# Toeplitz bias table and decay sums of a hybrid decoder block spread over partitions through memory instead of by products on TensorE

## The reference, cut to what matters

```python
rel = t_pos[None, :, None] - idx
bias = rel_bias[t5_bucket(rel)].astype(jnp.float32)
logits = logits + jnp.transpose(bias, (0, 1, 3, 2))
```

```python
cs = jnp.cumsum((dt * a).reshape(bsz, n_c, CHUNK, n_h), axis=2)
seg = cs[:, :, :, None, :] - cs[:, :, None, :, :]
decay_ls = jnp.exp(jnp.where(tri[None, None, :, :, None], seg, -jnp.inf))
scores = jnp.einsum("bclhn,bcshn->bclsh", ch, bh).astype(jnp.float32) * decay_ls
```

## Time and profile before

| | us |
|---|---|
| runs | 811.29, 812.05, 813.7 (median 812.05) |
| profiled execution, first to last instruction | 810.0 (its own time is not listed apart) |
| PE busy | 762.2 (94%) |
| DVE busy | 501.6 (62%) |
| ACT busy | 333.9 (41%) |
| POOL busy | 165.3 (20%) |

### The profile page before, as it was taken

The page is one execution under the profiler, slowest core; times in us unless marked ns, Lnnn a source line. Parts: engine busy times, 40 slices in busy tenths (PEclk is TensorE's granted clock), DMA queues, the critical chain, the costliest instruction groups (busy, mean ns, idle before and its releaser), DMA issues.

```text
span 810.0 us, 9558 instructions
## 1 busy us (share of the span) xinstructions
PE 762.2 (94%) x3406; PEld 595.6 (74%) x3406; DVE 501.6 (62%) x753; ACT 333.9 (41%) x491; POOL 165.3 (20%) x128
## 2 busy tenths in 40 slices
PE   3899999999899989979997999999999999999998
PEld 3567777766566667768885788888888888888886
DVE  4236789758779787988867366656655665322222
ACT  5244435465744648435233333443443334211110
POOL 2200433257556434432312000000000000000000
PEclk9999999999899989999998999999999999999999
DMA  8341132311111014111141133323333332322212
GB/s 254 123 155 58 53 104 53 104 53 52 53 52 53 2 52 156 53 53 53 52 131 53 52 104 104 103 83 81 95 104 104 104 104 98 109 104 90 72 47 104
DMA packets 78048, 69.47 MB, mean 86 GB/s; under 512 B 5815, under 2 KB 64535, under 8 KB 78015
## 3 DMA queue, kind: packets, MB, share of 16 engines
q1 hardware_dynamic: 77871, 68.51, 27.4%
q10 hardware_dynamic: 144, 0.52, 0.2%
HBM read 66.91 MB, written 2.12 MB: 85 GB/s over the span
## 4 chain that ended last, share of the span: by engine, by line
PE 79%; DVE 11%; issue 4%; ACT 3%; POOL 2%; DMA 1%; DVEq 0%; POOLq 0%; ACTq 0%
PE bank L1437 67%; PE bank L1443 3%; PE bank L1575 3%; PE bank L1594 2%; DVE u_acc L551 2%; DVE w_lo L561 2%; POOL stats L711 2%; DVE xbcT L1230 1%; PE bank L1552 1%; PE bank L1643 1%; DMA x_in<-in_x 1%; DVE h_lo L1073 1%; PE bank L1560 1%; PE bank L1617 1%; ACT xbcT L924 1%
## 5 line engine op out<-in xcount | busy, mean ns | idle before, releaser
L1437 PE MATMUL bank<-h_hi,w_hi 128*128 128x512 f32 x496 | 200.3, 404 | 1.8 <-DVE h_lo L1073 1.8
L1437 PE MATMUL bank<-h_lo,w_hi 128*128 128x512 f32 x496 | 196.0, 395 | 0.0
L1437 PE MATMUL bank<-h_hi,w_lo 128*128 128x512 f32 x496 | 195.4, 394 | 0.0
L561 DVE TENSOR_TENSOR w_lo<-w_raw,w_hi 128x1408 fp32r<-128x1408 f32 (+1 forms) x34 | 71.3, 2098 | 82.2 <-ACT w_hi L817 82.1
L1437 PEld LDWEIGHTS bank<-h_hi,w_hi 128*128 128x128 f32 x496 | 94.9, 191 | 36.9 <-issue 16.8
L1437 PEld LDWEIGHTS bank<-h_hi,w_lo 128*128 128x128 f32 x496 | 94.7, 191 | 20.4
L1437 PEld LDWEIGHTS bank<-h_lo,w_hi 128*128 128x128 f32 x496 | 95.0, 192 | 18.8
L1398 DVE SCALAR_TENSOR_TENSOR f<-bank,prm,f 128x511 f32<-128x511 f32 x88 | 65.8, 747 | 57.1 <-ACT f L1042 50.8
L817 ACT ACTIVATE w_hi<-w_raw 128x2048 fp32r<-128x2048 f32 x34 | 64.9, 1910 | 77.9 <-PE bank L1437 77.9
L551 DVE SCALAR_TENSOR_TENSOR u_acc<-u_in,prm,u_acc 128x511 f32<-128x511 f32 (+29 forms) x90 | 86.2, 996 | 0.7
L1042 ACT ACTIVATE f<-bank,prm 128x512 f32<-128x512 f32 x44 | 33.8, 769 | 101.2 <-PE bank L1437 101.2
(11 more groups left out here) (220 smaller groups left out, 1140.3 us busy)
## 6 DMA issues: line engine op xcount, KB each, us to landing
w_raw<-in_w_up SPq DMA_DIRECT2D x44, 512.0 KB, 4.5
w_raw<-in_w_in SPq DMA_DIRECT2D x34, 512.0 KB, 4.4
w_raw<-in_w_down SPq DMA_DIRECT2D x22, 512.0 KB, 4.2
w_raw<-in_w_out SPq DMA_DIRECT2D x12, 512.0 KB, 4.2
x_in<-in_x SPq DMA_DIRECT2D x4, 512.0 KB, 6.8
trev<-distance_table SPq DMA_DIRECT2D x1, 2048.0 KB, 8.2
x<-in_x SPq DMA_DIRECT2D x4, 512.0 KB, 6.5
out_x<-y_out SPq DMA_DIRECT2D x8, 256.0 KB, 2.0
```

The costliest lines, as they stand in the source:

```text
L561: eng.tensor_tensor(wlo[:, slot, cols], wraw[:, slot, cols], whi[:, slot, cols].bitcast(F32), ALU.subtract).then_inc(ready, 1)
L1437: ins = pe.matmul(o, a, b, start=first and i == 0 and q == 0, stop=last and i == n - 1 and q == 2)
```

## The change

The bias rows are now made on all 128 partitions at once: `relx` repeats each head's column 16 times (an ACT copy), the product is 128 rows tall, and ACT stores each partition's 640 values eight times, 128 x 8 x 640 (2.6 MB), from its own DMA queue. One read with a row step of NG - 1 from offset P - 1 gives the table the right way round, straight into `tbias` (2 MB, slot 9, issued by ACT). `trev`, `jrev`, the eight products and the eight copies go.

`cs` moves from slot 62 to slot 20, with a third product that gives the sums as rows (32 x 128); DVE copies them, ACT stores them (16 KB), and per chunk SP reads them back with a partition step of 0 (`csl`, 512 KB each) into `dec`, which is now doubled; `sct` is written over `dec`. The `csr` products go; the subtraction on DVE reads `dec` in SBUF instead of a bank.

The diff, cut to its core:

```diff
+CSL_SLOTS = (64, 64, 70, 74)
...
     put(1, ("gtab",))
-    for h in range(NH):
-        put(11 + h, ("tbias", h))
+    put(9, ("tbias",))
+    put(20, ("cs",))
...
-    put(s0, ("silux",), ("cs",))
+    put(s0, ("silux",))
...
+    for t, n in enumerate(CSL_SLOTS):
+        put(n, ("csl", t))
     for t, n in enumerate(SSD_SLOTS):
-        put(n, ("csr", t))
...
-                elif s[0] == "gtab":
...
-                    sp.dma_start(gdram, gsb[:, :]).then_inc(s_gout, 16)
-                    sp.wait_ge(s_gout, 16)
...
-                    src = bass.AP(gdram.tensor, 0, [[1, P], [NG, NH], [1, 512]])
-                    sp.dma_start(trev[:, :, :], src).then_inc(s_trev, 16)
+                elif s[0] == "csl":
+                    t = s[1]
+                    sp.wait_ge(s_cst, 16)
+                    if t < 2:
+                        finished(sp, "pv", NT - 1)
+                    else:
+                        finished(sp, "yd", t - 2)
+                    src = bass.AP(cdram.tensor, SH * P * t, [[0, P], [P, SH], [1, P]])
+                    sp.dma_start(dec[:, t % 2, :, :], src).then_inc(s_csr[t], 16)
...
                 elif k == "gtab":
+                    act.wait_ge(s_oneh, 32)
+                    act.activation(relx[:, :].rearrange("b (h c) -> b h c", h=NH),
+                                   relb[:, :].unsqueeze(2).to_broadcast([NBUCKET, NH, P // NH]),
+                                   ACT.Copy).then_inc(relx_ready, 1)
...
+                    act.dma_start(gdram, gsb[:, :].unsqueeze(1).to_broadcast([P, NH, NG]))\
+                        .then_inc(s_gout, 16)
...
                 elif k == "tbias":
-                    finished(act, *s)
-                    drain(act.activation(tbias[:, s[1], :], ps(*s)[:, :], ACT.Copy), *s)
+
+                    act.wait_ge(s_gout, 16)
+                    act.wait_ge(xn_ready, NT)
+                    src = bass.AP(gdram.tensor, P - 1, [[NG - 1, P], [P * NG, NH], [1, 512]])
+                    act.dma_start(tbias[:, :, :], src).then_inc(s_tbias, 16)
...
                 elif k == "cs":
                     act.wait_ge(csx_ready, 1)
                     act.activation(ecs, csx, ACT.Exp).then_inc(ecs_ready, 1)
+                    evacuated(act, "cs")
+                    act.dma_start(cdram, csT[:, :]).then_inc(s_cst, 16)
...
-                        d = dec[:, 4 * g:4 * g + 4, :]
-                        finished(dve, "csr", t, g)
+                        d = dec[:, t % 2, 4 * g:4 * g + 4, :]
+                        dve.wait_ge(s_csr[t], 16)
...
-                        drain(dve.tensor_tensor(
-                            d, ps("csr", t, g)[:, :].rearrange("p (h l) -> p h l", h=4),
-                            csx[:, c:c + 4].unsqueeze(2).to_broadcast([P, 4, P]), ALU.subtract),
-                            "csr", t, g)
-                        evacuated(dve, "csr", t, g)
+                        dve.tensor_tensor(d, d, csx[:, c:c + 4].unsqueeze(2).to_broadcast([P, 4, P]),
+                                          ALU.subtract).then_inc(segx_ready, 1)
...
-                elif k == "csr":
-                    t = s[1]
-                    for g in range(SG):
-                        claim(pe, "csr", t, g)
-                        for h in range(4):
-                            c = SH * t + 4 * g + h
-                            ins = pe.matmul(ps("csr", t, g)[:, P * h:P * h + P],
-                                            dta[:, c:c + 1].to_broadcast([P, P]), tri[:, :],
-                                            start=True, stop=True)
-                        ins.then_inc(aux_done, 1)
```

More of the change, by code:

```diff
@@ L241, in make_groups @@
         k = s[0]
-        if k in ("prm", "tbias", "idx", "score", "turn", "ln", "lnT", "qkT", "cs", "iwT",
+        if k in ("prm", "idx", "score", "turn", "ln", "lnT", "qkT", "cs", "iwT",
                  "yT"):
@@ L328, in build @@
     w_in, w_out, w_up, w_down = w_in[0], w_out[0], w_up[0], w_down[0]
-    gdram = nc.dram_tensor("distance_table", (NH, NG), F32, kind="Internal").ap()
+    gdram = nc.dram_tensor("distance_table", (P, NH, NG), F32, kind="Internal").ap()
+    cdram = nc.dram_tensor("decay_rows", (NT * SH, P), F32, kind="Internal").ap()
     with ExitStack() as ctx:
@@ L377, in build @@
         relb = at("relb", [NBUCKET, NH], F32, r7 + 2560)
-        gsb = at("gsb", [NH, NG], F32, r7 + 3 * K)
-        jrev = at("jrev", [P, P], F32, r7 + 6 * K)
-        trev = at("trev", [P, NH, 512], F32, r6)
+        gsb = at("gsb", [P, NG], F32, r7 + 3 * K)
+        relx = at("relx", [NBUCKET, P], F32, r7 + 7 * K)
         tbias = at("tbias", [P, NH, 512], F32, r2)
@@ L413, in build @@
         gssm = at("gssm", [P, 512], F32)
-        dec = at("dec", [P, SH, P], F32, rs)
-        sct = at("sct", [P, SH, P], F32, rs + 4 * K)
+        dec = at("dec", [P, 2, SH, P], F32, rs)
+        csT = at("csT", [NT * SH, P], F32, r7 + 6 * K)
         ssm_hi = at("ssm_hi", [P, 4, SEQ], F32R, r4)
@@ L472, in build @@
                              "head_params_landed", "onehot_landed"))
-        s_gout, s_trev, s_x2, s_yout, s_gm, s_gf = (
-            sem(n) for n in ("gtable_stored", "trev_landed", "x2_landed", "y_stored",
+        s_gout, s_tbias, s_x2, s_yout, s_gm, s_gf = (
+            sem(n) for n in ("gtable_stored", "tbias_landed", "x2_landed", "y_stored",
                              "gm_row_landed", "gf_row_landed"))
@@ L499, in build @@
         csx_ready, ecs_ready = sem("csx_ready"), sem("ecs_ready")
+        s_cst, relx_ready = sem("decay_rows_stored"), sem("relx_ready")
+        s_csr = [sem(f"decay_rows_landed{t}") for t in range(NT)]
+        segx_ready = sem("segx_ready")
         seg_ready, dec_ready, sct_ready = sem("seg_ready"), sem("dec_ready"), sem("sct_ready")
@@ L729, in _ @@
                         finished(pool, "qkT", "k", 3)
-                        for hh in range(NH):
-                            evacuated(pool, "tbias", hh)
+                        pool.wait_ge(s_tbias, 16)
                     if i >= 2:
@@ L840, in _ @@
                         n = 512 if i == 0 else NG - 512
[L841 removed]
+                        drain(act.activation(gsb[:, 512 * i:512 * i + n], ps("gt", i)[:, 0:n],
                                              ACT.Copy), "gt", i)
+                    for i in range(2):
+                        evacuated(act, "gt", i)
+                    act.dma_start(gdram, gsb[:, :].unsqueeze(1).to_broadcast([P, NH, NG]))\
+                        .then_inc(s_gout, 16)
                 elif k == "norm":
@@ L866, in _ @@
                     dst = {"iq": iqT, "v": v_tok, "z": z_tok, "cg": u_acc, "ca": u_in}.get(what)
+                    if (what, i) == ("ca", 3):
+                        act.wait_ge(s_cst, 16)
                     take(dst[:, i, :], what, i)
@@ L1498, in _ @@
                         n = 512 if i == 0 else NG - 512
-                        pe.matmul(ps("gt", i)[0:NH, 0:n], relb[:, :], oneh[:, 512 * i:512 * i + n],
+                        pe.wait_ge(relx_ready, 1)
+                        pe.matmul(ps("gt", i)[:, 0:n],
+                                  relx[:, :],
+                                  oneh[:, 512 * i:512 * i + n],
                                   start=True, stop=True).then_inc(aux_done, 1)
@@ L1642, in _ @@
                         c = slice(SP_ * h, SP_ * h + SP_)
-                        ins = pe.matmul(ps("yd", t)[:, c], sct[:, h, :], xd[:, c], start=True,
+                        ins = pe.matmul(ps("yd", t)[:, c], dec[:, t % 2, h, :], xd[:, c], start=True,
                                         stop=True)
```

40 lines of the change are left out of this document (12 added, 28 removed).

## The result

| | before | after |
|---|---|---|
| median of the runs | 812.88 us (4 runs, 811.29 to 814.04) | 824.23 us (4 runs, 822.16 to 825.19) |
| profiled execution: span | 810.0 us | 823.3 us |
| mean granted clock of it | 0.983 | 0.961 |

What follows compares the result with a forecast made beforehand. PE rarely stops up to 104 us, DVE sets the pace from 104 to 124 and bounds the scan. Terms -0.3 + 1.7 - 1.4 - 0.3 + 0.5 = +0.2 us on 812.05 gave 812.3 us, range 807.5 to 815.7.

Steps and rivals of the forecast that it cites:

- Term 1: Up to k's turn: eight products and copies leave, `cs` in slot 20 gives back 2.5 us; -0.3 us (-2.8 to +0.5).
- Term 2: At the wait for k: PE waits 5 us instead of 3.56, lower clock follows; +1.7 us (0 to +3.1).
- Term 3: Behind the SiLUs: ACT's exponential and its table load leave the chain; -1.4 us (-0.5 to -1.6).
- Term 4: In the scan: the decay products leave PE, mostly lengthening its waits; -0.3 us (0 to -7.2).
- Term 5: In the scan: DVE's subtraction reads SBUF twice, one more delay beside POOL; +0.5 us (0.1 to 2.4).
- rival D: In the scan: the subtraction stands until POOL's instruction ends, 2.4 us in place of 0.5; 814.2 us, chance 0.1.
- At nothing: Table and decay reads and stores, ACT's `relx` copy and POOL's dropped instructions: hidden or in idle time, no cost.
- C: Before q's turn: the new 3.3 us wait lowers the clock too; +3.1 us, 815.4 us, chance 0.17.
- B: Low-clock stretches fall elsewhere after a small shift, dropping one such as that after 216.62; 809.2 us, chance 0.13.
- A: At k: `cs` is covered and the clock holds; -4.0 us, 808.0 us, chance 0.2.

Runs made afterwards that it cites:

- e9: The changed kernel with POOL's waits of e5 and `cs` in slot 30 instead of 20, behind the normalised k; 816.40 us, ratio 1.0059.
- e5: The changed kernel with POOL's three instructions of the second, third and fourth chunk held until that chunk's `seg` is done; 815.92 us, ratio 1.0036.
- e17: The kernel before with one edit, `cs` moved to slot 20, table and decay still by products; 813.74 us, ratio 1.0009.
- e1: The table half of the change alone: bias table by memory, decay sums on PE as before; 813.57 us, ratio 1.0026.
- e4_cs22: The changed kernel with `cs` in slot 22 instead of 20; 817.52 us, ratio 1.0088.

## Why the prediction was wrong

- **Term 1** (-0.3): held as a sum. PE waited 3.34 us before q's turn, which began at 92.58 (said: 3.3 and 92.6), and DVE's scaling for k came at 112.89 (said: 112.8):

```profile
112.89 0.16 DVE L1205 TENSOR_SCALAR stats<-stats 128x32 f32<-128x32 f32 x1
112.96 2.28 DVE L564 TENSOR_TENSOR w_lo<-w_raw,w_hi 128x2048 fp32r<-128x2048 f32 x1
...
120.58 1.89 DVE L1213 TENSOR_TENSOR k_tok<-k_tok,stats 128x512 f32<-128x512 f32 x3 [1.97 <-POOL stats L709]
```

  Its inner piece, 2.5 us for `cs`, is 2.2 by e9 against e5 (112.29 and 114.49). `cs` on ACT is as worked out: exponential, issue, copy, square.

```profile
108.58 0.28 ACT L974 ACTIVATE stats<-stats 128x96 f32<-128x96 f32 x1 [5.74 <-DVE stats L1254]
108.59 0.34 ACTq L976 DMA_DIRECT2D decay_rows<-csT  x1
108.97 0.60 ACT L913 ACTIVATE k_tok<-bank 128x512 f32<-128x512 f32 x1
109.60 0.60 ACT L916 ACTIVATE sq<-bank 128x512 f32<-128x512 f32 x1
```

- **Term 2** (+1.7): the mechanism held, the size was 2.4. PE went on at 123.13 after 4.77 us, 0.24 earlier than before, and slot 28 stands 2.21 later.
- **Term 3** (-1.4): held, -1.3 between slots 60 and 64.
- **Term 4** (-0.3, bounds 0 and -7.2) failed, in its bound. "That wait becomes 3.6 and DVE gains nothing" was right: it became 3.79. But a wait that grows was costed at nothing, a few paragraphs after I had costed one at k by the clock. In the first chunk of the profiled execution it cost 4.3 us (slot 69 at -3.66, slot 70 at +0.65), of which 1.8 is the gain that had to go and the rest the lower level behind the wait. A loss belonged into the range; e17 shows that even an unchanged wait can have it.
- **Term 5** (+0.5, bounds 0.1 and 2.4) is the step that decided: it measured 4.25 us of DVE in `seg`, and holding POOL back was worth 8 us of the time (e5), clock included. I took "one more such delay" from a single long L1257, where rival D counted one delay of 0.8 in each of three chunks. The rule that D rested on was right and D's size was not: it used one POOL instruction for each chunk, while POOL has four in a row, and three of the fourth chunk's four `seg` instructions were caught (+2.8 us; +0.7 in the second and third chunk, as D had it). The `yb` row of 1.52 in the earlier trace rows, directly ahead of `seg`, was the second witness. And D costed DVE's delay one for one: it had no term for the clock, by which PE's work in the scan took some 15 us more.
- **"At nothing"**: the reads landed in time (5.5 to 9.7 us each, and DVE never waits for one); right.
- **Rivals.** C's wait before q's turn left the clock alone in the changed kernel, and lowered it in e1, e5 and several others (3.4 us near 93). B's shift was seen (before, stretches of 6.8, 3.4 and 6.8 us at 217, 265 and 292 us; after, 3.4 and 10.2 us at 221 and 265: -2.7 us between slots 28 and 60). A didn't come. D was the right case; I gave it a chance of 0.1 and 2.4 us, and it was worth 8. That terms 1 to 3 came out within a microsecond says nothing for the forecast: what decided lay behind them.

## What to carry to other kernels

Before an operand is moved from PSUM to SBUF on DVE, list what POOL does at that moment, and look for DVE instructions that are already twice as long as their twins: each two-input one ended a fixed time after POOL's here, and a burst of POOL work catches several in turn. Where the move must be made, hold POOL's work by one semaphore wait, or fuse two DVE passes into one. And work that was taken from an engine which waits for another was worth nothing here (7.2 us of products gone, 7.1 us more of waiting); give such a term a loss too.

## What the runs showed of the hardware

- A DVE instruction of 128x512 with two SBUF inputs, 0.69 us alone (0.75 for `yb`), ends 0.55 us after the POOL instruction during which it began (fourteen cases in the scan, six before and eight after, 0.53 to 0.55 us); POOL's own next one is stretched from 1.04 to 1.49. One with a bank as input keeps its 0.68 beside POOL.
- One instruction that subtracts a scalar of each partition and adds a mask takes 0.34 us for 128x128, from a bank as from SBUF. In a row each begins 0.26 us after the last: eight are through in 2.18 us, 0.56 us less than four passes of 128x512.
- In the profiled executions the stretches at 1.2 GHz last 3.4, 6.8, 10.2 or 13.7 us, and near-identical waits were followed by one or not. The kernel before varied from 0.966 to 0.985 in its mean clock with unchanged code, and e4_cs22 had two groups of runs 9 us apart. The Trainium skill, "TensorE: Matmul & The Clock Gate", "What's actually happening", says that the chip's look at PE's activity runs freely and isn't tied to the kernel; that agrees with a wait whose effect changes from trace to trace.
